# One dense 128x256 product ahead of TensorE's wait for a unit's weights, in the eight differential sample units

## What is computed

```python
proj = einsum("btd,de->bte", h, w_in)            # 3072 columns: sb q,k,v and diff q,k,v
# stick-breaking attention, 8 heads of 64:
#   A[t,s] = sigmoid(z_ts) * prod_{s<j<t} (1 - sigmoid(z_tj))
# differential attention, 4 heads, two maps each, values of 128:
z = einsum("bqhcd,bkhcd->bchqk", q, k) * scale - slopes * dist
p = softmax(z, axis=-1);  a = p[:, 0] - lam * p[:, 1]
out = einsum("bhqk,bkhe->bqhe", a, v)            # then rms norm, w_out
x = layer_norm(DEEP * x + mix_out, ln1_g, ln1_b)
# experts: 4 of 32 for each of the 320 tokens, softmax over the 4 logits
gu = xb @ w_gate_up[e] + b_gate_up[e]            # 1024 x 2048, clamped SwiGLU
y += gate * (hid @ w_down[e] + b_down[e])        # 1024 x 1024
x = layer_norm(DEEP * x + ffn, ln2_g, ln2_b)
```

## Time and profile before

| what | value |
|---|---|
| time, median of 3 runs | 1404.84 us |
| the three runs | 1403.28, 1404.84, 1419.48 us |
| the profiled execution, its own time | 1417.58 us |
| its span, first to last instruction | 1415.7 us |
| mean granted TensorE clock in it | 0.966 |
| TensorE busy | 1277.5 us, 90% of the span |
| mean HBM traffic | 359 GB/s |

### The profile page before, as it was taken

How to read it: one execution, slowest core, us unless ns; L and a number is a source line. 1 busy time by engine, 2 the same in 40 slices (tenths; PEclk the granted TensorE clock), 3 DMA queues, 4 the chain that set the end, 5 groups by cost and what they waited for, 6 DMA issues and landing times.

```text
span 1415.7 us, 19452 instructions
## 1 busy us (share of the span) xinstructions
PE 1277.5 (90%) x7204; PEld 482.1 (34%) x7205; DVE 442.5 (31%) x781; ACT 236.2 (17%) x572; POOL 125.1 (9%) x155
## 2 busy tenths in 40 slices
PE   8899997988989999998888889999988999988884
PEld 6355444554532332222222222333222233222221
DVE  0244454654742222211121222223121323112116
ACT  1323335743231000000000000000000001000001
POOL 2022233410000000000000000000000000000000
PEclk9999998987989999999999999999999899999997
DMA  9559689786169999999999998899999999999992
GB/s 360 209 197 357 223 330 363 274 336 223 54 244 400 416 417 416 417 417 418 418 418 416 416 418 349 348 418 417 417 418 416 416 416 418 418 417 418 416 416 81
DMA packets 99718, 508.07 MB, mean 359 GB/s; under 512 B 10413, under 2 KB 10797, under 8 KB 64858
## 3 DMA queue, kind: packets, MB, share of 16 engines
q1 hardware_dynamic: 85298, 431.15, 75.2%
q0 software_dynamic: 14240, 76.03, 13.9%
q10 hardware_dynamic: 136, 0.28, 0.1%
HBM read 501.92 MB, written 5.24 MB: 358 GB/s over the span
## 4 chain that ended last, share of the span: by engine, by line
PE 26%; DMA 20%; SPq 17%; DVE 5%; issue 2%; ACT 1%; ACTq 0%; DVEq 0%; POOLq 0%; POOL 0%
DMA arena<-in_w_gate_up 20%; SPq L269 17%; PE psum L2006 12%; PE psum L2036 9%; PE psum L1976 2%; DVE arena L2163 1%; PE psum L2024 1%; DVE arena L2159 1%; DVE arena L2155 1%; DVE arena L2156 1%; PE psum L2057 1%; SPq L1933 0%; DVE arena L2218 0%; DVE arena L2215 0%; PE psum L1968 0%
## 5 line engine op out<-in xcount | busy, mean ns | idle before, releaser
L2006 PE MATMUL psum<-arena 128*64 128x512 f32 x2112 | 494.8, 602 | 63.2 <-DMA arena<-in_w_gate_up 61.0
L2006 PEld LDWEIGHTS psum<-arena 128*64 128x64 f32 x2112 | 137.0, 137 | 413.1 <-issue 217.9
L2129 DVE SCALAR_TENSOR_TENSOR arena<-psum,arena 64x512 f32<-64x512 f32 (+2 forms) x132 | 130.7, 1009 | 437.7 <-PE psum L1976 437.2
L2036 PE MATMUL psum<-arena 128*64 128x512 f32 x1056 | 236.5, 601 | 0.7 <-ACT arena L2096 0.7
L2036 PEld LDWEIGHTS psum<-arena 128*64 128x64 f32 x1056 | 73.5, 138 | 161.0 <-issue 131.6
L2084 ACT ACTIVATE arena<-psum 128x512 f32<-128x512 f32 x34 | 20.3, 597 | 595.3 <-PE psum L1968 595.3
L2155 DVE TENSOR_SCALAR arena<-psum 128x512 f32<-128x512 f32 x33 | 22.8, 692 | 304.6 <-PE psum L2006 304.6
L1976 PE MATMUL psum<-arena 64*128 64x512 f32 (+1 forms) x396 | 109.7, 632 | 0.9 <-ACT arena L2100 0.9
L1947 POOL COPY small_i<-small_i 128x1 int32 (+1 forms) x34 | 6.2, 183 | 983.7 <-PE psum L1968 875.1
L1192 DVE STREAM_TRANSPOSE arena<-arena 128x1024 f32<-128x1024 f32 x64 | 74.9, 1214 | 1.8 <-DVE arena L1296 0.7
L581 PE MATMUL psum<-arena 128*128 128x512 f32 x128 | 64.9, 641 | 3.6 <-DVE arena L1181 3.6
(11 more groups left out here) (245 smaller groups left out, 930.8 us busy)
## 6 DMA issues: line engine op xcount, KB each, us to landing
arena<-in_w_gate_up SPq DMA_DIRECT2D x256, 1024.0 KB, 23.5
arena<-in_w_down SPq DMA_DIRECT2D x128, 1024.0 KB, 25.0
arena<-in_w_in SPq DMA_DIRECT2D x12, 1024.0 KB, 20.6
arena<-in_w_out SPq DMA_DIRECT2D x4, 1024.0 KB, 10.2
out<-arena SPq DMA_DIRECT2D x12, 256.0 KB, 2.0
arena<-in_x_prompt SPq DMA_DIRECT2D x4, 512.0 KB, 5.2
arena<-in_b_gate_up ACTq DMA_DIRECT2D x68, 4.0 KB
arena<-in_ln_g SPq DMA_DIRECT2D x2, 512.0 KB, 6.0
```

Of the source, the lines that this page charges most:

```text
L2006: ins = nc.tensor.matmul(psum[64 * h:64 * h + 64, n, :], x_k, slot[k][:, col:col + 512], start=False, stop=(k == KD - 1))
L2036: ins = nc.tensor.matmul(psum[64 * h:64 * h + 64, 4, :], h_k, slot[s][:, col:col + 512], start=(k == 0), stop=(k == KD - 1))
L2129: ins = nc.vector.scalar_tensor_tensor(out=r, in0=psum[0:nt, banks[h]:banks[h] + at_once, :], scalar=item_gate[0:nt, b, col], in1=r, op0=A ...
```

## The change

A product is put ahead of the wait for `w_ready` in `turn_weights`, in units 8 to 15 alone. Its stationary operand is the identity, its moving operand the first 256 columns of the constant table, and it writes the first 256 columns of `W_BANK`, which the transposes behind it overwrite. Nothing reads its result.

```diff
                     y, b = UNITS[u]
                     side = side_of(u)
+                    if y:
+                        nc.tensor.matmul(psum[:, W_BANK, 0:QUARTER], ident, tab[:, 0:QUARTER], start=True, stop=True)
                     pe.wait_ge(w_ready, u + 1)
                     for h in range(2):
```

## The result

The changed kernel takes 1401.2 us, the median of 16 runs (1397.63 to 1404.61), against 1412.47 us for the kernel before in 16 runs (1400.78 to 1423.52). The time forecast, 1405.3 us, and its sign were wrong. The median before that the forecast stood on, 1404.84, came from three executions; 16 of them have their median 7.6 us higher. In those 16, ten are over 1408 us; of the changed kernel, none. The fastest executions are 3 us apart (1397.63 and 1400.78), and the six of the kernel before under 1408 us have a median of 1403.8, 2.6 us above that of the changed kernel. So most of the gain is that a long kind of execution is gone.

A forecast was written before the change was run, and what follows sets the result against it. Bound: the expert stage's weight stream, movable only by its start; TensorE nearly bounds the first block's units. Median 1404.84 plus 0.32 (unit 14) and 0.14 (unit 15), the rest hidden, gave 1405.3 us; range 1397 to 1419.

The forecast's parts named there:

- The bound and the way a gain is handed on: Expert stage: weight stream of some 970 us; a microsecond won or lost in the first block is one of the total.
- The direct cost: Units 8 to 15: product mostly hidden in gaps before line 711, adding 0.46 us; bounds 0 and 4.7.
- rival 1: End of first block: product in unit 14 or 15 keeps or restores full clock, 6 us faster, 1399 us; chance 0.13.
- the hole: 223.8 to 234 us: TensorE busy only 4.72 of 10.2 us, read as an instruction block late behind the gathers.
- the fall at 309 us: Clock at one half from about 309 to 329 us, in the first block; put at 5.8 us lost.
- Rival 2: Units 8 to 15: added instructions shift block borders, so most executions have a late instruction block, 1418 us; chance 0.18.
- rival 3: Units 8 to 15: no gap covers the product, 8 x 0.59 us at the most, 1409.5 us; chance 0.05.
- the mark of 12.6 within 0.1 us: Units 8 to 15: sign of a right forecast, the period of a unit staying within 0.1 us of 12.6.

The follow-up runs named there:

- the kernel before, second profile: The kernel before, run again with no edit for a second profile and its clocks by execution: 1410.66 us over 10 executions, ratio 0.9977.

## Why the prediction was wrong

- **The bound and the way a gain is handed on** were right: 1002.8 us from the first loads to the end in both profiles.
- **The direct cost** was right in result and loose in working. Hidden in the units with a gap: yes (1.79 us both times). Measured from unit 9 to unit 15 it is 0.2 us for seven products (74.96 against 74.76), where 0.46 was put for eight. Unit 14: no gap, the cost put at 0.32; lines 709 to 713 there are 289.22 to 289.75, 0.53. The step misread "x2": the two matmuls are the two halves of one product, so line 665's 0.64 us was one product, not two, and the product at hand takes 0.48 to 0.53. It still fits into 0.69. This is also why the program has 32 instructions more, not 16, and why the profile shows 16 matmuls where 8 were forecast.
- **The step that failed is in rival 1**: "no unit from 10 to 13, where six of the eight products go, has lost it, so there is nothing to win". The gain from a held clock in the units was put at nothing on that ground. It was read from one execution, in which the clock happened to hold in those units. In 61 of 105 executions of the kernel before the time is over 1408 us, nearly all at a low mean clock, and the two profiles of such executions without a whole product show falls in four units running, 4.5 us for each of three. The premise was also miscounted: units 10 to 13 hold four of the eight products. Six is the number with units 8 and 9, and unit 9 did show half clock in the prediction's own rows, which it laid to the hole. Rival 1 had the right mechanism in the wrong place: it looked to the fall at 309 us, which the product does not avert (0.51 after, as 0.52 before); the product of unit 15 ran in that stretch, 1.15 us at half clock, and did not bring the clock back. That its 1399 us lies near the measured 1401.2 is luck. It had a chance of 0.13.
- **The median.** 1404.84 us was the middle of three, two of the short kind and one of the long. The spread of 16 us stood in the prediction, and was laid to the hole. The hole (4.72 us busy in 10.2) is in none of the other 13 profiles. The profiled execution before, 1417.58 us at a clock of 0.966, is long mostly without the clock; only one of the 105 is like it (1415.11 at 0.966). The long kind is the clock's. What the hole was stays open: the 8-column product refutes only that shifted instructions bring the gain.
- **Rival 2 and rival 3** did not come. The one expected 1418 us from a hole, the other a cost in every unit. The period stayed at 12.80 us from unit 10 to 11, as before; the mark of 12.6 within 0.1 us fits the units from 11 to 13, which took 12.6 both times.
- **The range**, 1397 to 1419, holds the time because it was drawn to take in both kinds of execution, not for its reasons, and within 2% was right; but what was forecast was no change, and the ratio is clear of 1. With the time of the kernel before held at the better of its two kinds, a change that removes the worse one was outside what the sum could show.

The Trainium skill (TensorE: Matmul & The Clock Gate, section A second HAM failure mode: psum-queue depth-cycling) tells of a kernel that idles briefly between groups of matmuls, often enough for the clock to go to and fro. The traces here agree in that the clock goes to and fro once in each of four units with a gap of 0.69 us. The gap alone does not do it: with the product behind the wait the same gap is idle and the clock stays up. The Trainium skill (the same page, section What's actually happening) has activity release the throttle; the prediction gave that half credit, and so do the runs: a product more in a unit kept the clock up, and 20.51 us busy out of 20.74 at the end of the block did not bring it back.

## What to carry to other kernels

When executions of one kernel spread in two groups, compare their mean granted clocks before looking at anything else, and don't take one profile, or three times, for the kernel. In a unit that repeats with TensorE nearly busy the clock can still fall, in unit after unit; a product in a gap that is there anyway can buy the short kind of execution for next to nothing. Put it ahead of the wait, count each fp32 product as two matmuls, and ask whether it fits: the same product without a gap cost 0.4 us a unit.

## What the runs showed of the hardware

- The clock fell to half in four units running though none of them has a gap over 0.69 us (the kernel before, second profile, and the product of 8 columns). In a unit where it held TensorE was busy 11.68 of 12.79 us.
- One more fp32 product of 256 columns in each of these units ends that: 0 of 28 executions of the changed kernel over 1408 us, against 61 of 105. With 16 of the 128 stationary columns loaded it is 0 of 12, with 8 moving columns 5 of 12. Single falls still come, as at 213.6 us (0.53).
- Once down the clock can stay down under a busy TensorE: 20.51 of 20.74 us busy at 0.51, 12.8 of them in matmuls with 16 stationary columns or 64 rows.
- A microsecond at half clock costs this kernel 0.39 us over whole executions, and 4.5 us for a fall of 10.0 to 10.4 in a unit. Work of TensorE alone, done at half the clock, would lose 0.5; that other engines and transfers share the path is a reading, not shown.
- An fp32 product of 128x256 is two matmul instructions, together 0.48 to 0.53 us at full clock and 1.15 at half.
